# Two-block transformer on one core: products side by side at the stage seams, single modulation tiles through two buffers, layer-norm moments tile by tile

## The chip, the cores and the metric

The kernel runs on one core of a Trainium2 chip. The metric is the device time of one execution in microseconds (us). Engines: PE is TensorE (matmuls), PEld its weight loads, DVE is VectorE, ACT is ScalarE, POOL is GpSimd, SP is SyncE, which here only issues transfers.

## The reference

Two transformer blocks in a row on x of 512 tokens by 1024 features, in float32. The first (two layers) has sparse indexed attention, banded attention, gates and a gated feed-forward; the second has forgetting attention, a multi-scale pool, a state-space mixer, and 16 routed experts. What the change touches:

```python
for l in range(DEPTH):                                   # DEPTH = 2
    mod = c_act @ w_ada[l] + b_ada[l]                    # 6 x 1024 modulation values
    sh_m, sc_m, gt_m, sh_f, sc_f, gt_f = jnp.split(mod, 6, axis=-1)
    h = rms_norm(x, g_mix[l]) * (1.0 + sc_m[:, None]) + sh_m[:, None]
    z = h @ w_in[l] + b_in[l]                            # q, k, v, indices, gates ga, gb
    merged = jax.nn.sigmoid(ga) * y_a + jax.nn.sigmoid(gb) * y_b
    x = x + gt_m[:, None] * (merged @ w_out[l])
    h2 = rms_norm(x, g_ffn[l]) * (1.0 + sc_f[:, None]) + sh_f[:, None]
    gate, up = jnp.split(h2 @ w_gu[l], 2, axis=-1)
    x = x + gt_f[:, None] * ((jax.nn.silu(gate) * up) @ w_down[l])
# second block
h = layer_norm(x) * (1.0 + sc_m) + sh_m
mix = hybrid_mixer(h, ...)                               # attention, pool, ssd, gates, w_out
x = layer_norm(ALPHA * x + g_m * mix, ln_mix_g, ln_mix_b)
h = layer_norm(x) * (1.0 + sc_f) + sh_f
ffn = grouped_moe(h, w_router, ...)
x = layer_norm(ALPHA * x + g_f * ffn, ln_ffn_g, ln_ffn_b)
```

## The kernel before, in words

All activations lie transposed: a tile is 128 features (partitions) by 512 tokens, and x, h and merged have eight tiles each (KC = 8). The program is written out by hand, one instruction stream per engine, with semaphores between them; nothing is scheduled by a planner. The classes `Plan` only number the products, weight units and sums, so that each engine knows what count to wait for.

**Products.** A float32 product is made from three fp32r matmuls per chunk of 128 features: upper weight half by upper h, upper by lower, lower by upper (`passes`, lines 583 to 585). A full product has 8 chunks, 24 matmuls of 128x128 by 512 columns. Products go to two PSUM banks in turn, `lin[p % 2]`; `bank_for(p)` waits until product p-2 was evacuated (`lin_free`). ACT or DVE evacuate.

**Weights.** SP loads one unit of 512 KB (a weight of 1024 by 128) into one of four slots of `ring`; unit n waits until the product that read unit n-4 has ended (line 504). ACT writes the upper half (`upper`, line 1236), POOL the lower half (line 2416), and a product waits for `w_lower`. SP's queue is in order: what waits there holds all behind it.

**Modulation.** `mod` is a vector by matrix product, done on DVE: a tile of 128 by 1024 weights is loaded by SP into `wada` and reduced against `csil` (`modulate`, line 1731). In the gates (8 turns), and in the attention outputs of the second block (8 turns, `attout`), SP loads two tiles at a time, 1 MB (`load_tiles`, line 509), into one buffer, so a load waits until DVE has read the one before. Four tiles belong to a turn. In gate/up one tile belongs to each of the first 16 turns.

**A turn of the gates** has two products of h (gates ga, gb; 24 matmuls each) and two of 12 matmuls (attention outputs). ACT evacuates the first two (line 1309), DVE the third and fourth (lines 2004, 2007), adds them into `merged` (line 2010), then reads the tiles. DVE writes the lower half of merged one turn later (line 1826).

**Seams.** Before mix, gate/up and fd, DVE scales a tile of x, ACT applies gain and shift twice (upper half and whole), and DVE takes the difference (`h_lo`, line 1756); the first product waits for it chunk by chunk. The output products wait in the same way for the last tile of merged.

**Layer norms of the second block** (`layer_norm`): sums of x over the features by eight matmuls with ones (line 623), the mean, centring on DVE, squares of the centred tiles on ACT (line 1472), eight more sums, a root on ACT (line 1248), a reciprocal and scaling on DVE (lines 1761, 1763), an affine step on ACT (line 1264). ln1 stands between the two blocks, ln2 and ln3 between the output products and the router (line 1080, 32 groups of matmuls with h as the stationary operand and 16 columns), ln4 at the end, followed by one store of the output.

Of the kernel before, what the change touches and what calls it, by code (L numbers as in the profile page):

```python
# [9 lines left out]
ACT = mybir.ActivationFunctionType  # L10
# [4 lines left out]
P = 128  # L15
# [76 lines left out]
def att_finished(s):  # L92
# [15 lines left out]
    ("ln1", 1, dict(aux=2)),  # L108
# [7 lines left out]
    ("ln2", 1, dict(aux=2)),  # L116
    ("ln3", 1, dict(aux=2)),
    ("router", 1, dict(aux=5)),
    ("ln4", 1, dict(aux=2)),
# [7 lines left out]
class Stream:  # L127
# [13 lines left out]
    def tiles(self, n):  # L141
        self.ada.append((self.slot(n * D), n))
# [130 lines left out]
def two_blocks(nc, w_all, vec1_all, vec2_all, consts, x_in, pos_in, cond, rel, out):  # L273
    ctx = ExitStack()
    with ctx:
# [206 lines left out]
        def _(sp):  # L482
# [34 lines left out]
            for layer in range(LAYERS):  # L517
                load(LAYER.at("gates", "unit", 0))
                for t in range(8):
                    load(3)  # L520
                    if t == 0:
                        sp.wait_ge(o_free, LAYER.at("mix", "o", 1, layer))
                    load_tiles()
                    load_tiles()
                load(8)
                for t in range(FF_T):
                    load(2)
                    if t < 16:
                        load_tiles()
                load(24)  # L530
            load(25)
            for t in range(8):
                load(2)
                if t == 0:
                    sp.wait_ge(o_free, SECOND.at("att", "o", 8))
                load_tiles()
                load_tiles()
            load(20 + 40 + 16 + 8 - 3)
# [23 lines left out]
        def _(pe):  # L562
# [37 lines left out]

            def half_of_h(p, u, part):
# [15 lines left out]
            def column_sum(a, src, k, ready=None):  # L617
# [6 lines left out]
                if k == KC - 1:  # L624
                    mm.then_inc(aux_full, 1)

# [47 lines left out]
            for layer in range(LAYERS):  # L674
# [60 lines left out]
                make("ka", split)  # L735
                make("ki")
# [124 lines left out]
                for t in range(8):  # L861
                    ready = (lambda k: (sem("m_split"), layer * KC + k + 1)) if t == 0 else None
                    product(at("out", "lin", t), [(at("out", "unit", t), 0, chunks_of(mg_hi, mg_lo, range(KC), ready))])
# [4 lines left out]
                for t in range(FF_T):  # L868
# [1824 lines left out]
```

## Time and profile before

| What | Value |
|---|---|
| Median of three runs | 3703.48 us (3698.95 to 3704.59) |
| Profiled execution, its own time | 3694.89 us |
| Span of its profile | 3693.2 us |
| Mean granted TensorE clock | 0.933 |
| Busy: PE, PEld, DVE, ACT, POOL | 86%, 65%, 41%, 28%, 29% |
| Chain that ended last: PE, DVE, DMA, ACT | 48%, 14%, 5%, 3% |

A row of the timeline gives start, duration, engine, line, operation, output and input; in brackets how long the engine had been idle and who ended that. Clock 1.00 is 2.4 GHz, 0.50 is 1.2 GHz. Matmuls overlap, so their starts (0.227 us apart at full clock) tell more than their durations. The stages of layer 0 lie at 58 to 972 us (gates 372 to 515), of layer 1 at 981 to 1906 (gates 1300 to 1450), the second block from there: attention to 2177, attention outputs to 2285, pool to 2436, ssd to 2788, ssd outputs to 2943, output products to 2987, norms and router to 3063, experts to 3622, combination and last norm to 3693.

### The profile page before, as it was taken

What the parts mean: (1) busy time and instruction counts of PE and PEld (TensorE: products, weight loads), DVE (VectorE), ACT (ScalarE), POOL (GpSimd) and SP (SyncE); (2) the same over time, 40 slices, a digit from 0 to 9 for tenths busy, and PEclk for the clock granted to TensorE, in tenths of its full rate; (3) what the DMA queues carried; (4) which work ended last, traced back from release to release, by engine and by line L of the source; (5) the groups of instructions that cost most, each with busy time, mean ns of one, the idle gap of its engine ahead of it and who ended that gap; (6) DMA issues with size and microseconds to landing.
All of it is one profiled execution on the core that took longest, in us unless ns stands there. A gap on an engine that the chain in (4) does not pass through costs nothing.

```text
span 3693.2 us, 38767 instructions
## 1 busy us (share of the span) xinstructions
PE 3183.1 (86%) x15370; PEld 2406.2 (65%) x15370; DVE 1507.0 (41%) x2585; ACT 1045.4 (28%) x1639; POOL 1059.1 (29%) x523
## 2 busy tenths in 40 slices
PE   4887988999898688899989987788888975999994
PEld 2654766887665466688756766666664545888882
DVE  5776543211267645221124434568782141010003
ACT  3444223223344422322234431233331121000002
POOL 1330333444333033344425523334441111000001
PEclk9997999999999899999999998899999986999997
DMA  5210553433311076243323226233332204989982
GB/s 199 60 41 12 182 184 96 144 113 101 105 57 44 12 280 215 86 145 118 98 81 90 79 94 210 66 103 94 95 97 69 97 17 180 338 329 334 337 329 103
DMA packets 176966, 501.73 MB, mean 136 GB/s; under 512 B 18401, under 2 KB 100449, under 8 KB 159409
## 3 DMA queue, kind: packets, MB, share of 16 engines
q1 hardware_dynamic: 153984, 415.14, 33.5%
q0 software_dynamic: 13344, 49.84, 3.5%
q10 hardware_dynamic: 9488, 34.71, 2.7%
q8 instruction: 99, 1.62, 0.2%
q14 instruction: 51, 0.41, 0.0%
HBM read 464.36 MB, written 35.29 MB: 135 GB/s over the span
## 4 chain that ended last, share of the span: by engine, by line
PE 48%; DVE 14%; DMA 5%; ACT 3%; issue 2%; POOL 0%; DVEq 0%; POOLq 0%; SPq 0%; ACTq 0%
PE banks L1123 9%; PE banks L583 9%; PE banks L585 8%; PE banks L584 8%; PE banks L1145 4%; PE banks L1065 3%; DMA arena<-in_w_all 3%; DVE abuf L2188 2%; PE banks L623 2%; DVE arena L1731 1%; DMA ring<-in_w_all 1%; PE banks L648 1%; PE banks L669 1%; DVE arena L1923 1%; PE banks L658 1%
## 5 line engine op out<-in xcount | busy, mean ns | idle before, releaser
L2416 POOL TENSOR_TENSOR w_lo<-ring,w_hi 128x1024 fp32r<-128x1024 f32 (+2 forms) x363 | 878.8, 2425 | 1609.9 <-ACT w_hi L1236 1609.5
L584 PE MATMUL banks<-h_lo,w_hi 128*128 128x512 f32 x2104 | 838.9, 399 | 0.0
L583 PE MATMUL banks<-hx_hi,w_hi 128*128 128x512 f32 (+1 forms) x1400 | 591.9, 423 | 66.0 <-DVE h_lo L1756 36.9
L585 PE MATMUL banks<-hx_hi,w_lo 128*128 128x512 f32 (+1 forms) x1400 | 558.4, 399 | 0.0
L1236 ACT ACTIVATE w_hi<-ring 128x1024 fp32r<-128x1024 f32 (+2 forms) x363 | 375.9, 1037 | 529.2 <-DMA ring<-in_w_all 507.4
L584 PEld LDWEIGHTS banks<-h_lo,w_hi 128*128 128x128 f32 x2104 | 403.4, 192 | 93.6 <-issue 9.7
L583 PEld LDWEIGHTS banks<-hx_hi,w_hi 128*128 128x128 f32 (+1 forms) x1400 | 270.7, 193 | 176.2 <-issue 79.0
L1123 PE MATMUL banks<-abuf,ring 128*128 128x128 f32 x2944 | 334.7, 276 | 1.4 <-DVE abuf L2366 0.9
L1123 PEld LDWEIGHTS banks<-abuf,ring 128*128 128x128 f32 x2944 | 332.5, 193 | 1.9 <-issue 1.9
L585 PEld LDWEIGHTS banks<-hx_hi,w_lo 128*128 128x128 f32 (+1 forms) x1400 | 269.5, 192 | 61.2 <-issue 0.7
L583 PE MATMUL banks<-hf_hi,w_hi 128*128 128x512 f32 x704 | 279.6, 397 | 24.6 <-DVE h_lo L1756 24.6
L585 PE MATMUL banks<-hf_hi,w_lo 128*128 128x512 f32 x704 | 279.5, 397 | 0.0
L1731 DVE CUSTOM_DVE_ANT_0 arena<-arena 128x1024 f32<-128x1024 f32 x144 | 207.1, 1438 | 161.6 <-DMA arena<-in_w_all 153.2
L1309 ACT ACTIVATE sgs<-banks 128x512 f32<-128x512 f32 x84 | 50.0, 595 | 543.5 <-PE banks L585 496.2
L2033 DVE TENSOR_TENSOR arena<-sgs,banks 128x512 f32<-128x512 f32 x44 | 30.2, 687 | 372.6 <-PE banks L585 372.6
L583 PEld LDWEIGHTS banks<-hf_hi,w_hi 128*128 128x128 f32 x704 | 132.7, 189 | 63.2 <-issue 22.8
L1145 PE MATMUL banks<-arena,abuf 128*128 128x512 f32 x368 | 161.8, 593 | 1.0 <-DMA arena<-in_w_all 1.0
L585 PEld LDWEIGHTS banks<-hf_hi,w_lo 128*128 128x128 f32 x704 | 133.0, 189 | 30.7
L2510 POOL DMA_DIRECT2D made<-abuf x23 | 12.3, 536 | 475.2 <-DVE abuf L2377 475.2
L2020 DVE SCALAR_TENSOR_TENSOR x<-banks,mod,x 128x512 f32<-128x512 f32 x32 | 24.0, 751 | 301.3 <-PE banks L585 301.3
L583 PE MATMUL banks<-hid_hi,w_hi 128*128 128x512 f32 x352 | 143.0, 406 | 3.6 <-DVE hid_lo L2041 3.6
L2377 DVE COPY abuf<-banks 128x512 f32<-128x512 f32 x23 | 15.9, 691 | 301.7 <-PE banks L1145 301.7
(366 smaller groups left out, 4495.9 us busy)
## 6 DMA issues: line engine op xcount, KB each, us to landing
ring<-in_w_all SPq DMA_DIRECT2D x340, 512.0 KB, 3.8
ring<-in_w_all SPq DMA_DIRECT2D x46, 2048.0 KB, 8.1
arena<-in_w_all SPq DMA_DIRECT2D x27, 2048.0 KB, 8.6
arena<-in_w_all SPq DMA_DIRECT2D x48, 1024.0 KB, 4.9
arena<-in_w_all SPq DMA_DIRECT2D x32, 512.0 KB, 4.9
routed<-abuf POOLq DMA_DIRECT2D x1, 12288.0 KB, 47.7
abuf<-routed POOLq DMA_DIRECT2D x24, 512.0 KB, 8.4
made<-abuf POOLq DMA_DIRECT2D x23, 512.0 KB, 7.9
```

The lines of the kernel that those rows point to most:

```text
L583: pe.matmul(bank[0:m, :], upper, hi, start=first, stop=False)
L584: pe.matmul(bank[0:m, :], upper, lo, start=False, stop=False)
L585: return pe.matmul(bank[0:m, :], lower, hi, start=False, stop=last)
L623: mm = pe.matmul(aux, ones, src(k), start=(k == 0), stop=(k == KC - 1))
L1065: mm = pe.matmul(bank, raw_w[(u + 1) % SLOTS][:, k * P:(k + 1) * P], yT[:, k, :], start=(k == 0), stop=(k == 15))
L1123: mm = pe.matmul(bank[:, ct * P:(ct + 1) * P], w[:, k * E_FF + ct * P:k * E_FF + (ct + 1) * P], xT[par][:, k * P:(k + 1) * P], start=(k == ...
L1145: mm = pe.matmul(sc_b[half], hidb[:, k * P:(k + 1) * P], wdown[:, k * D + half * SEQ:k * D + (half + 1) * SEQ], start=(k == 0), stop=(k == 3))
L1236: act.activation(w_hi[s][:, 0:n], raw_w[s][:, 0:n], ACT.Copy).then_inc(w_upper, 1)
L1309: act.activation(sg[n][:, :], lin[p % 2], func, bias=bias).then_inc(lin_free[p % 2], 1)
L1731: mine(dve.tensor_tensor_reduce(w, w, csil, 1.0, 0.0, MUL, ADD, mod_sum[:, n:n + 1]))
L2188: ins = STT(o, c[:, tap:tap + SEQ], gpar(5 * t + tap), o, MUL, ADD)
L2416: pool.tensor_tensor(w_lo[s][:, 0:n], raw_w[s][:, 0:n], w_hi[s][:, 0:n], ALU.subtract)\
```

## The change

- `side_by_side` makes two products chunk by chunk, into both banks, where the first product of a stage waited for its input tiles: mix (ka, ki), output (0, 1), gate/up (0, 1), fd with the first attention product, and the output of the second block. It waits for both banks first.
- `load_tile` loads one modulation tile (512 KB) at a time into one of two halves of `wada`, each with its own semaphore. SP's order changes: in the gates a tile is issued behind each weight load. DVE reads two tiles of a turn ahead of the evacuations of the third and fourth product and two behind; the sum goes straight to `mod`, without the extra addition. The last tile of merged is lowered ahead of the last two reads.
- The layer norms take variance as mean of squares less squared mean; sums of x and of its squares are made tile by tile, as x becomes ready (in ln1 between the down products, in ln2 between the output products, in ln3 as the affine step of ln2 gives tiles), the second sum in the bank `ob`. DVE centres and scales tile by tile.
- The router's logits are made with w_router as the stationary operand, 16 by 512, copied, and turned by four transposes.
- The load of ACT's square-root table, the load and silu of the next c, stand earlier, between output products; the result is stored tile by tile.

```diff
@@ sync
-            def load_tiles():
-                n, ((at, size), tiles) = next(ada)
-                sp.wait_ge(sem("wada_free"), n - 3)
-                sp.dma_start(wada[:, 0:tiles * D], w_all[at:at + size * P].rearrange("(p n) -> p n", p=P))\
-                    .then_inc(sem("wada_in"), 16)
+            def load_tile():
+                n, ((at, size), i) = next(ada)
+                n -= 4
+                if n >= 2:
+                    sp.wait_ge(sem("wada_free"), n - 1)
+                sp.dma_start(wada[:, n % 2 * D:(n % 2 + 1) * D], w_all[at:at + size * P].rearrange("(p n) -> p n", p=P)[:, i * D:(i + 1) * D])\
+                    .then_inc(sem("wada_in%d" % (n % 2)), 16)
@@ gates
+                load(3)
+                sp.wait_ge(o_free, LAYER.at("mix", "o", 1, layer))
+                load_tile()
+                load_tile()
                 for t in range(8):
-                    load(3)
-                    if t == 0:
-                        sp.wait_ge(o_free, LAYER.at("mix", "o", 1, layer))
-                    load_tiles()
-                    load_tiles()
-                load(8)
+                    load()
+                    load_tile()
+                    load()
+                    load_tile()
+                    load()
+                    if t < 7:
+                        load_tile()
+                        load_tile()
+                load(5)
@@ attention outputs
+            load(2)
+            sp.wait_ge(o_free, SECOND.at("att", "o", 8))
+            load_tile()
+            load_tile()
             for t in range(8):
-                load(2)
-                if t == 0:
-                    sp.wait_ge(o_free, SECOND.at("att", "o", 8))
-                load_tiles()
-                load_tiles()
+                load()
+                load_tile()
+                load()
+                load_tile()
+                if t < 7:
+                    load_tile()
+                    load_tile()
@@ tensor
+            def side_by_side(p, u, chunks, widths=(P, P)):
+
+                pe.wait_ge(w_lower, STREAM.units[u + 1][4])
+                pair = [bank_for(p), bank_for(p + 1)]
+                for k, (hi, lo, ready) in enumerate(chunks):
+                    for n, m in enumerate(widths):
+                        mm = passes(pair[n], u + n, k * m, m, (hi, lo, None if n else ready), k == 0, k == KC - 1)
+                        if k == KC - 1:
+                            mm.then_inc(lin_full[(p + n) % 2], 1)
...
-            layer_norm("ln2", 1)
-            layer_norm("ln3", 2)
-            pe.wait_ge(sem("h_ready"), KC)
+                for k in ([t - 1] if t < 7 else [6, 7]):
+                    column_sum(at("ln2", "aux"), lambda k: x[:, k, :], k, lambda k: pe.wait_ge(sem("x_mixed"), k + 1))
+                    square_sum(lambda k: moe[:, k, :], k, lambda k: pe.wait_ge(sem("moments"), k + 1))
+            for k in range(KC):
+                column_sum(at("ln3", "aux"), lambda k: x[:, k, :], k, lambda k: pe.wait_ge(sem("x_affine"), k + 1))
+                square_sum(lambda k: merged2[:, k, :], k, lambda k: pe.wait_ge(sem("moments"), KC + k + 1))
@@ vector, gates
+                    modulate_beside(16 + 4 * t, v1)
+                    modulate_beside(17 + 4 * t, v1)
                     taken(dve, p)
                     produced(dve, p + 2)
                     TT(tmp[:, :], sg[0][:, :], lin[(p + 2) % 2], MUL).then_inc(lin_free[(p + 2) % 2], 1)
...
-                    modulate_beside(16 + 4 * t, 2, v1)
-                    modulate_beside(18 + 4 * t, 2, v1)
-                lower_merged(layer * KC, mg_lo, merged, mg_hi, 7)
+                    if t == 7:
+                        lower_merged(layer * KC, mg_lo, merged, mg_hi, 7)
+                    modulate_beside(18 + 4 * t, v1)
+                    modulate_beside(19 + 4 * t, v1)
```

DVE in a turn of the gates, before (mg_lo is the lower half of merged, the ISA rows with arena are the reads of modulation tiles, tmp and sgs take the third and fourth product):

```order
L1826 TENSOR_TENSOR mg_lo_63<-arena,mg_hi_62 128x512 [waits m_upper,dve_steps]
L2004 TENSOR_TENSOR tmp<-sgs,banks 128x512 [waits lin_full1,lin_free1]
L2007 TENSOR_TENSOR sgs<-sgs,banks 128x512 [waits lin_full0,lin_free0]
L2010 TENSOR_TENSOR arena<-tmp,sgs 128x512 [waits lin_free0,lin_free1]
L1731 ISA arena<-arena 128x1024 [waits wada_in]
L1731 ISA arena 128x1
L1731 ISA arena<-arena 128x1024 [waits dve_steps]
L1731 ISA arena 128x1
L1737 TENSOR_TENSOR mod<-arena,vec 128x2 [waits dve_steps]
```

The same turn in the change:

```order
L1906 TENSOR_TENSOR mg_lo_63<-arena,mg_hi_62 128x512 [waits dve_steps,m_upper]
L1806 ISA arena,mod<-arena,vec 128x1024 [waits wada_in0]
L1806 ISA mod 128x1
L1806 ISA arena,mod<-arena,vec 128x1024 [waits dve_steps,wada_in1]
L1806 ISA mod 128x1
L2086 TENSOR_TENSOR tmp<-sgs,banks 128x512 [waits dve_steps,lin_full1,lin_free1]
L2089 TENSOR_TENSOR sgs<-sgs,banks 128x512 [waits lin_full0,lin_free0]
L2092 TENSOR_TENSOR arena<-tmp,sgs 128x512 [waits lin_free0,lin_free1]
L1806 ISA arena,mod<-arena,vec 128x1024 [waits wada_in0]
L1806 ISA mod 128x1
L1806 ISA arena,mod<-arena,vec 128x1024 [waits dve_steps,wada_in1]
L1806 ISA mod 128x1
```

Two of the four reads, and their waits for the tiles, now stand between mg_lo and the evacuation of the third product (tmp); the additions into mod are gone.

SP around the same turn, before (ring is a weight unit, arena a load of modulation tiles; lin_full is the end of the product that frees the slot):

```order
L504 DMA ring<-in_w_all 128x1024 [waits lin_full0]
L504 DMA ring<-in_w_all 128x1024 [waits lin_full1]
L504 DMA ring<-in_w_all 128x1024 [waits lin_full0]
L509 DMA arena<-in_w_all 128x2048 [waits wada_free] x2
L504 DMA ring<-in_w_all 128x1024 [waits lin_full0]
```

The same place in the change:

```order
L505 DMA ring<-in_w_all 128x1024 [waits lin_full0]
L512 DMA arena<-in_w_all 128x1024 [waits wada_free] x2
L505 DMA ring<-in_w_all 128x1024 [waits lin_full0]
L512 DMA arena<-in_w_all 128x1024 [waits wada_free]
L505 DMA ring<-in_w_all 128x1024 [waits lin_full1]
L512 DMA arena<-in_w_all 128x1024 [waits wada_free]
L505 DMA ring<-in_w_all 128x1024 [waits lin_full0]
```

Single tiles stand behind each weight load, and two behind the third, which waits for the second product of a turn.

SP at the end of the gates in the change (128x8x128 are the units of the output products):

```order
L505 DMA ring<-in_w_all 128x8x128 [waits lin_full0]
L512 DMA arena<-in_w_all 128x1024 [waits wada_free]
L505 DMA ring<-in_w_all 128x8x128 [waits lin_full1]
L512 DMA arena<-in_w_all 128x1024 [waits wada_free]
L505 DMA ring<-in_w_all 128x8x128 [waits lin_full0]
```

The last tile is issued behind the weight that waits for output product 0 (lin_full1).

## Rows read from the trace of the kernel before

**Rows 1.** Waits of PE by releaser: total us, times, longest.

```profile
PE banks L583 <- DVE h_lo L1756: 61.4, 23, 16.3
PE banks L583 <- DVE pooled_lo L2157: 30.5, 4, 13.1
```

**Rows 2.** Windows by stage: length, busy of each engine (instructions), clock, DMA share, GB/s.

```profile
2247.30:2254.92 7.62, 7.62 (x25) 6.10 (x26) 2.62 (x5) 0.00 (x0) 1.52 (x1) 0.72 0.40 153
384.53:510.08 125.55, 117.63 (x506) 95.28 (x505) 81.87 (x95) 32.62 (x40) 49.98 (x20) 0.99 0.57 203
1306.25:1444.50 138.25, 120.74 (x505) 96.72 (x505) 79.16 (x95) 32.62 (x40) 49.65 (x20) 0.95 0.71 266
510.08:539.21 29.13, 18.31 (x73) 14.63 (x73) 10.97 (x20) 6.49 (x8) 10.03 (x4) 0.82 0.67 230
2197.40:2285.56 88.16, 72.53 (x290) 57.93 (x289) 40.98 (x62) 15.73 (x18) 28.29 (x12) 0.90 0.56 201
```

**Rows 3.** Timeline of PE: ends of products in gates and attention outputs, next starts.

```profile
473.24 0.39 PE L584 MATMUL banks<-h_lo,w_hi 128*128 128x512 f32 x1
473.46 0.39 PE L585 MATMUL banks<-hx_hi,w_lo 128*128 128x512 f32 x1
...
480.82 0.50 PE L583 MATMUL banks<-hx_hi,w_hi 128*128 128x512 f32 x1 [1.53 <-DVE tmp L2004]
...
2247.30 0.79 PE L583 MATMUL banks<-att_hi,w_hi 128*128 128x512 f32 x1 [4.51 <-DVE arena L2122]
```

**Rows 4.** Landings: lone weight 473.9; tiles in gate/up; weights 2206.4; 1 MB (page).

```profile
DMA to landing us min/median/max: 3.5/3.5/3.5
...
DMA to landing us min/median/max: 4.2/4.8/5.1
...
DMA to landing us min/median/max: 5.8/6.2/6.6
...
arena<-in_w_all SPq DMA_DIRECT2D x48, 1024.0 KB, 4.9
```

**Rows 5.** Timeline of DVE and POOL: tile reads, evacuation, a lower weight half.

```profile
473.43 1.22 DVE L1731 CUSTOM_DVE_ANT_0 arena<-arena 128x1024 f32<-128x1024 f32 x1
...
480.09 0.67 DVE L2004 TENSOR_TENSOR tmp<-sgs,banks 128x512 f32<-128x512 f32 x1
...
1540.91 2.38 POOL L2416 TENSOR_TENSOR w_lo<-ring,w_hi 128x1024 fp32r<-128x1024 f32 x1 [1.18 <-ACT w_hi L1236]
...
1542.24 2.14 DVE L1731 CUSTOM_DVE_ANT_0 arena<-arena 128x1024 f32<-128x1024 f32 x1 [0.18 <-DVE arena L2033]
```

**Rows 6.** Timeline at the entry to gate/up, layer 1: ACT, then PE.

```profile
1514.14 1.28 ACT L1433 ACT_TABLE_LOAD   x1
1516.51 1.28 ACT L1248 ACT_TABLE_LOAD   x1
...
1524.93 0.77 PE L583 MATMUL banks<-hf_hi,w_hi 128*128 128x512 f32 x1 [10.58 <-DVE h_lo L1756]
...
1540.87 0.39 PE L585 MATMUL banks<-hf_hi,w_lo 128*128 128x512 f32 x1
```

**Rows 7.** Timeline at the entry to mix, layer 1: first product's end, head root.

```profile
991.87 0.40 PE L585 MATMUL banks<-hx_hi,w_lo 128*128 128x512 f32 x1
...
999.29 0.59 ACT L1253 ACTIVATE rstd<-banks 128x512 f32<-128x512 f32 x1
```

**Rows 8.** Chain of waits, in order of time: start, us, what.

```profile
1909.59 8.81 PE banks L623 x16
...
2988.73 7.15 PE banks L623 x16
...
3007.74 3.37 DVE rstd L1761
...
3049.26 13.85 PE banks L1080 x64
...
3657.54 9.01 PE banks L623 x16
```

More of the change, by code:

```diff
@@ L141, in tiles @@
     def tiles(self, n):
-        self.ada.append((self.slot(n * D), n))
+        slot = self.slot(n * D)
+        self.ada += [(slot, n)] if n == 4 else [(slot, i) for i in range(n)]
     def unit(self, last, *copies, raw=False):
@@ L733, in index_scores @@
                         mm.then_inc(sem("ix_full"), 1)
-                make("ka", split)
-                make("ki")
+                side_by_side(lin_of("ka"), at("mix", "unit"), of_h(split))
                 head_norm("ka")
@@ L860, in _ @@
                     product(p + 3, [(u + 2, 4 * P, chunks_of(attb_hi, attb_lo, range(4)))])
-                for t in range(8):
-                    ready = (lambda k: (sem("m_split"), layer * KC + k + 1)) if t == 0 else None
-                    product(at("out", "lin", t), [(at("out", "unit", t), 0, chunks_of(mg_hi, mg_lo, range(KC), ready))])
+                side_by_side(at("out", "lin"), at("out", "unit"),
+                             chunks_of(mg_hi, mg_lo, range(KC), lambda k: (sem("m_split"), layer * KC + k + 1)))
+                for t in range(1, 8):
+                    if t > 1:
+                        product(at("out", "lin", t), [(at("out", "unit", t), 0, chunks_of(mg_hi, mg_lo, range(KC)))])
                     for k in ([t - 1] if t in range(1, 7) else [6, 7] if t == 7 else []):
@@ L1774, in layer_norm, with centre @@
                 read(dve, a)
[L1775 to L1778 removed]
+                mine(TT(rstd[:, :], tmp[:, :], tmp[:, :], MUL))
+                dve.wait_ge(sem("var_full"), n + 1)
+                mine(STT(rstd[:, :], ob, 1.0 / D, rstd[:, :], MUL, SUB))
+                tell(TS(rstd[:, :], rstd[:, :], 0.0, LN_EPS, MAX, ADD), sem("var_done"))
+                def centre(k):
+                    TT(dst[:, k, :], x[:, k, :], tmp[:, :], SUB).then_inc(sem("centred"), 1)
+                centre(0)
+                dve.wait_ge(sem("root_done"), n + 1)
+                mine(dve.reciprocal(rstd[:, :], rstd[:, :]))
+                for k in range(KC):
+                    if k + 1 < KC:
+                        centre(k + 1)
+                    dve.wait_ge(sem("centred"), n * KC + k + 1)
+                    TT(dst[:, k, :], dst[:, k, :], rstd[:, :], MUL).then_inc(sem("scaled"), 1)
+                    if lower is not None and k >= 2:
+                        lower(k - 2)
+                if lower is not None:
+                    lower(KC - 2)
+                    lower(KC - 1)
             def rotate(a, src, dst):
```

189 lines of the change are left out of this document (112 added, 77 removed).

## The prediction

> **What bounds the kernel now.** I read the engine that waits first. The page's waits of TensorE say who ends its idle time: at the seams between stages it stands until the first split tiles of h are written (61.4 us over 23 waits), and in the pooling stage for VectorE (30.5 us) [rows 1]. Then the windows by stage: in the gates of layer 0, turns 1 to 7, TensorE is busy 117.6 of 125.5 us at a clock of 0.99; in those of layer 1 120.7 of 138.3, with one long DMA of zeros beside it; from the last turn's second product to the end of the second output product only 18.3 of 29.1; in the attention outputs 72.5 of 88.2 at 0.90 [rows 2]. So there is something to win at the seams and in the attention outputs, and little in the gates, where almost any new wait is a loss.
>
> **The gates (term 1).** The modulation tiles are read by VectorE. Their transfers stand on SP behind weight loads that wait for a product to end. In the new order, tiles 4t and 4t+1 are issued behind a weight load that waits for the *second* product of turn t (call its end B), and VectorE reads both *before* it evacuates the third product. The first product of the next turn needs that bank. Before, tiles stood on SP at the same place, but VectorE read them after the evacuation.
>
> Before, B ended at 473.46 + 0.39 = 473.85 and the next turn began at 480.82 [rows 3]: 7.0 us, of which 5.4 are the third and fourth product (24 matmuls at 0.227, the step of the same rows) and 1.5 a wait.
> Now, from B = 0:
> - SP issues the weight at 0.0 and, at 0.4 an issue (my estimate), the first tile at 0.4; the second waits on the read of tile 4t-1, at about 0.8. A 512 KB load alone lands in 3.5 us; a tile behind a weight in 4.8; two weights behind a tile of 1 MB land 5.8 and 6.6 after their issue [rows 4]. So: weight 3.5, first tile 5.2, second 6.3.
> - ScalarE writes its upper half in about 1.1 and GpSimd lowers it in 2.38, from 4.8 to 7.2.
> - A tile's read takes 1.22, but 2.14 when it starts at 1542.24 while GpSimd works from 1540.91 to 1543.29: it ends 1.1 after GpSimd does. The evacuation, which takes one operand from PSUM, keeps its 0.67 [rows 5]. So the first read ends at 8.3, the second at 9.6, the evacuation at 10.4; the next turn begins at 10.5. The halves of the last merged tile are made before the first tile lands and hide in this.
> - TensorE stands 10.5 - 5.4 = 5.1 us. After 4.5 us of standing, the product at 2247.30 ran at a clock of 0.72 and took 7.6 instead of 5.5 [rows 2, 3]: 2.1 more.
>
> Per turn 10.5 - 7.0 + 2.1 = +5.6. A turn becomes 23.8 us. Layer 0: 7 x 23.8 = 166.6 against 125.5, **+41**. Layer 1: 166.6 against 138.3 is +28, and the zeros share the DMA engines as before; what they cost before is 138.3 - 125.5 = 12.8, of which I take 8: **+36**. Ends: without a read behind GpSimd the second read ends at 7.6 and the turn begins at 8.4, +1.4 a turn and no clock loss (+10 and +4 with the zeros); or +8 a turn if both reads wait.
>
> The Trainium skill ("SBUF — State Buffer", section "SBUF: two separate sides") says that VectorE with two SBUF inputs and GpSimd take the shared port pair in turn, each for a whole instruction. By that rule the second read may also be shut out, if GpSimd gets in between; the trace shows one such wait per read at most.
>
> **Behind the gates (term 2).** The two output products start when both banks are free, 11.2, run 48 matmuls in 11.2 + 2.1 and end at 24.5; before, the second ended at 29.1 [rows 2]. But the last tile is issued on SP behind the weight of output 4, which waits for output 0. It lands about 4.9 after the pair, its read takes 1.3, and the residual of output 0 is queued behind it on VectorE, then its square on ScalarE, then the column sum. TensorE stands 7.6 and loses 2.1 again. 24.5 + 7.6 + 2.1 + 1 = 35 against 29.4: **+5.8** per layer, +12 in all (from +1, when the pair starts at 9.2, to +12).
>
> **Entry to gate/up (3).** Table loads of 1.28 and the silu of c stand between the last sum and the root; they end 3.65 after they begin; hoisted, the first product starts 3.4 earlier. Tiles of h come every 1.41 us, six matmuls take 1.37, so both products end about 13.2 after the start, against 1541.26 - 1524.93 = 16.3 [rows 6]. **-6.3** per layer, -13 (ends: -8, -14). The Trainium skill ("ScalarE: Activation LUTs", section "What ACT_TABLE_LOAD costs") puts a switch at about 2.66 us with its drain; here the next instruction starts right behind the 1.28, so the trace decides; by the page two hoists would give 2.8 more.
>
> **Entry to mix (4).** The pair saves 2.9 us of TensorE, but the slot of the first product is freed 2 us later (before at 992.3 [rows 7]), its next weight lands 3.5 later, and ScalarE splits that weight before the head root (before at 999.29): it would start at 998.8. The pair's gain waits there: **-1** for both layers (0 to -3).
>
> **Layer norm 1 (5).** Eight square sums (8.81) and the squares leave the chain at 1909.59 [rows 8]; 5.4 come back between the down products. VectorE now centres and scales per tile, 2.0 us a tile instead of 1.41, but fd and the first attention product share that time. The next stage then stands on ScalarE, which empties the bank of that product only behind the fd chain. Estimate **-9** (-4 to -14).
>
> **Layer norms 2, 3, router (6).** From 2988.73 to the end of the logits at 3063.10 it is 74.4 us: four rounds of sums, two reciprocals of 3.37, the logits 13.85 [rows 8]. The first two rounds move between the output products (+12.9 there, of which 1.4 is the pair's wait for a bank and 1 the wait for x). What is left behind the last product: 6.2 to the root, 3.4, eight tiles; third and fourth round together 16 (16 sums at 0.89 to 1.1), behind them 2.7, 3.4, eight tiles at 1.25 with the logits beside them, 2 for copy and transposes: about 47. 76 - 47 - 13 = **-16** (-10 to -20).
>
> **Layer norm 4 (7).** The sums begin with the first x tile, 5 us before 3657.54 [rows 8]; output leaves per tile: 3693 becomes 3688, **-5** (-2 to -8).
>
> **Attention outputs and pooling (8).** Before, one buffer of 1 MB made a turn 14.7 (88.2/6) [rows 2]. Now the second tile of each turn waits on SP for that turn's first product; tracing tile by tile with landings of 3.5 to 5 and one GpSimd wait per turn I get turns of 10.9 and 15.9 in alternation, 13.4: **-8** (-16 to +4). The last read ends 8 us earlier, so of the 13.1 at the first pooling wait [rows 1] **-8** (-4 to -9). The Trainium skill ("DMA: Bandwidth & Descriptors", section "Measured") advises transfers of 1 MiB and more; here a half takes 3.5 against 4.9 for the whole [rows 4], and by that rule alone, four halves one after the other with their reads (4 x 4.8) would make a turn of 19, which only the second buffer avoids.
>
> Sum: 41 + 36 + 12 - 13 - 1 - 9 - 16 - 5 - 8 - 8 = +29. The profiled execution took 3694.9, 8.6 below the median of the runs shown (3703.5). So 3724 by the profile, **3733** by the median.
>
> **The rivals.**
> - *The gates' reads do not meet GpSimd, and the idle stays short of what lowers the clock.* Then terms 1 and 2 are 10 + 4 + 1 = +15, and the sum is -45: 3659. Decisive: whether the second tile's read ends before about 7.7 after B. For it: 1.5 us of standing never lowered the clock in these gates (0.99). Against it: GpSimd's work is released by the weight issued just ahead of the tiles, so the two meet each turn.
> - *The norms do not pay.* VectorE takes 2.0 us per tile where ScalarE set 1.41, and the sums are still read last; terms 5 to 7 halve and the attention outputs stay at 14.7: +29 + 15 + 8 = +52, 3756.
> - *The terms cancel.* If the gates cost half (+40 in all), the sum is about -20 to 0; a little of this lies within 0.2%.
>
> **How the numbers follow.** Forecast (slower by 15 to 45) 0.50; norms do not pay 0.12; reads do not meet, and all between it and the forecast on the fast side, 0.30; within 0.2% (7 us, about what a measurement of this kernel can tell from none) 0.08. So faster 0.30, same 0.08, slower 0.62. The range takes in most of the fast rival and the slow one: 3665 to 3768. The likeliest case alone spans 3718 to 3748.
>
> **What would show it.** In the gates of the changed profile: turns near 23.8 us; TensorE's wait for tmp near 5 us, some fifteen times, with a lower clock; reads of 2 us or more beside GpSimd; a wait of 7 to 8 us after the output pair. At gate/up, a root without a table load ahead of it. From the last output product to the logits near 47 us. I am wrong if the turns stay under 19.5 us: then term 1 falls, and the kernel is faster.

## The result, and the profile after

The changed kernel takes 3764.4 us (median of 4 runs, 3756.4 to 3769.0) against 3701.2 for the kernel before in the same series. The ratio is 1.0172, 95% interval 1.0156 to 1.0187: **slower by 63 us**, where I forecast slower by 30. The sign was right. The time lies inside the stated 3665 to 3768 us, but near its upper end and outside the band of 3718 to 3748 that I called likeliest: about half of the loss was missing from my sum. The profiled execution has a span of 3767.4 us against 3693.2, +74.2.

The waits of TensorE come first, as in [rows 1] (columns: total us, times, longest). I call one such wait a stand.

```profile
PE banks L599 <- DVE tmp L2086: 84.4, 14, 10.8
PE banks L599 <- DVE h_lo L1819: 48.9, 5, 15.4
...
PE banks L599 <- DVE sgs L2089: 24.5, 2, 12.6
PE banks L599 <- DVE pooled_lo L2242: 22.7, 4, 7.0
...
PE banks L649 <- ACT h L1463: 19.1, 4, 9.1
PE banks L599 <- POOL w_lo L2504: 18.6, 2, 12.3
...
PE banks L599 <- DVE arena L2205: 16.3, 4, 4.2
```

The seams shrank (61.4 to 48.9) and so did pooling (30.5 to 22.7). The wait for tmp, the evacuation of the third product of a gates turn, is 84.4 us in 14 waits. Three waits are new and large: 24.5 us ahead of the two output pairs (L2089), 8.8 and 9.1 of the 19.1 us behind them (L1463), and 12.3 of the 18.6 us for a lower weight half (L2504). The first of these stands in place of one that the kernel before had, 10.8 and 10.1 us of output product 0 for the last tile of merged:

```profile
PE banks L583 <- DVE mg_lo L1826: 20.9, 2, 10.8
```

The windows by stage (length, busy time by engine, clock, DMA share, GB/s): gates of layer 0 and of layer 1 from the end of turn 0 to the end of turn 7, then a stretch of the attention outputs with the first products of pooling.

```profile
391.74:560.82 169.08, 132.37 (x504) 105.82 (x504) 76.61 (x84) 32.93 (x41) 49.30 (x21) 0.86 0.47 154
1364.56:1543.95 179.39, 131.65 (x504) 105.25 (x504) 74.62 (x84) 34.08 (x42) 49.89 (x21) 0.84 0.57 206
...
2292.00:2395.00 103.00, 86.51 (x355) 69.43 (x354) 61.63 (x64) 19.79 (x23) 38.94 (x15) 0.94 0.66 227
```

The same seven turns took 125.5 us at 0.99 and 138.2 at 0.95 before [rows 2]. TensorE now runs the same products in 132 us instead of 118, at a granted clock of 0.86, and stands for the rest.

Where the 74 us arise, by the time at which the same product starts or ends in both traces (forecast: what my terms put there):

| from ... to | before ends at | after ends at | change | forecast |
|---|---|---|---|---|
| start to end of gates turn 0, layer 0 | 389.97 | 391.74 | +1.8 | -0.5 |
| gates turns 1 to 7 | 515.50 | 560.82 | **+43.5** | +41 |
| to the first gate/up product | 590.50 | 646.09 | **+10.3** | +2.4 |
| to mix of layer 1 | 981.49 | 1033.66 | -3.4 | -2.9 |
| to end of gates turn 0, layer 1 | 1311.69 | 1364.56 | +0.7 | -0.5 |
| gates turns 1 to 7 | 1449.90 | 1543.95 | **+41.2** | +36 |
| to the first gate/up product | 1524.93 | 1629.19 | **+10.2** | +2.4 |
| to the fourth attention product's end | 1971.76 | 2074.31 | -1.7 | -11.9 |
| to the first attention output product | 2179.18 | 2282.95 | +1.2 | 0 |
| to the last attention output product's end | 2285.56 | 2384.74 | -4.6 | -8 |
| to the first pooled product | 2316.72 | 2413.31 | -2.6 | -8 |
| to the end of the logits | 3063.10 | 3142.57 | -17.1 | -16 |
| to the end | 3693.2 | 3767.4 | -5.3 | -5 |

The gates, router and norm 4 came as forecast within a few us. Four places did not: twice between gates and gate/up, once at the forget seam (fd), once between the attention outputs and pooling.

A turn of the gates, in the chain of waits (start us, us, what):

```profile
483.99 5.43 DMA arena<-in_w_all
...
489.44 2.28 DVE arena L1806
...
491.91 1.28 DVE arena L1806
...
493.42 0.70 DVE tmp L2086
```

Tile, long first read, short second read, evacuation, next turn: the row that the forecast drew. The next turn starts 10.6 us after the second product's end (483.61 to 494.17), forecast 10.5.

The last turn is different. The chain from its second product to the first column sum:

```profile
556.00 10.86 DMA arena<-in_w_all
566.88 3.27 DVE arena L1806
...
570.34 1.28 DVE arena L1806
...
572.46 0.69 DVE sgs L2089
...
586.32 5.40 DMA arena<-in_w_all
591.74 1.28 DVE arena L1806
...
593.58 0.76 DVE x L2103
594.37 0.64 ACT h L1463
```

The tile takes 10.86 us, twice that of other turns. ScalarE's queue shows what shares the DMA engines with it (timeline of ACT, same turn):

```profile
555.55 0.35 ACTq L1456 DMA_DIRECT2D x<-in_x_in  x1
```

That is the 2 MB load of x back from HBM, issued half a microsecond before the tile. It stood at the same place in the program before, but no evacuation waited for the tile then. My working never looked at ScalarE's queue.

The forget seam (timeline of ACT, POOL and PE):

```profile
2009.59 1.06 ACT L1269 ACTIVATE w_hi<-ring 128x1024 fp32r<-128x1024 f32 x1 [3.23 <-DMA ring<-in_w_all]
...
2043.52 0.56 POOL L2540 DMA_DIRECT2D f_rows<-arena  x1 [35.21 <-DVE arena L2146]
2045.68 1.12 POOL L2545 DMA_DIRECT2D arena<-f_rows  x2 [1.60 <-DMA f_rows<-arena]
2046.81 2.35 POOL L2504 TENSOR_TENSOR w_lo<-ring,w_hi 128x1024 fp32r<-128x1024 f32 x1
...
2049.31 0.77 PE L599 MATMUL banks<-hx_hi,w_hi 128*128 128x512 f32 x1 [12.29 <-POOL w_lo L2504]
```

The upper half of the weight of attention product 1 is ready at 2010.7. GpSimd could lower it then, but first in its queue stands a wait for the fd rows, 35 us long. Product 0 was moved ahead of that chain by the pair; product 1 stands behind it, and the first four products end no earlier.

### The profile page after: what moved, and what is told of

The parts are those of the page before. It is cut to its first block, busy times and chain, and to the rows that moved or that the text cites. A ratio compares the mean times of both kernels' runs of the same rounds, so it can differ in the third digit from the quotient of the medians.

```text
span 3767.4 us, 38674 instructions
## 1 busy us (share of the span) xinstructions
PE 3207.1 (85%) x15326; PEld 2422.0 (64%) x15326; DVE 1510.8 (40%) x2518; ACT 1045.5 (28%) x1639; POOL 1056.2 (28%) x523
## 4 chain that ended last, share of the span: by engine, by line
PE 67%; DVE 19%; DMA 6%; ACT 4%; issue 3%; POOL 1%; SPq 0%; DVEq 0%; ACTq 0%; POOLq 0%
PE banks L599 15%; PE banks L601 14%; PE banks L600 14%; PE banks L1154 8%; DMA arena<-in_w_all 5%; PE banks L1176 4%; PE banks L1087 3%; DVE arena L1806 2%; DVE abuf L2273 2%; PE banks L649 1%; DVE arena L2003 1%; PE banks L681 1%; PE banks L702 1%; DVE arena L2002 1%; PE banks L662 1%
## 5 line engine op out<-in xcount | busy, mean ns | idle before, releaser
L2504 POOL TENSOR_TENSOR w_lo<-ring,w_hi 128x1024 fp32r<-128x1024 f32 (+2 forms) x363 | 876.7, 2417 | 1723.9 <-ACT w_hi L1269 1723.4
L600 PE MATMUL banks<-h_lo,w_hi 128*128 128x512 f32 x2104 | 850.7, 404 | 0.0
L599 PE MATMUL banks<-hx_hi,w_hi 128*128 128x512 f32 (+2 forms) x1400 | 607.4, 434 | 148.5 <-DVE tmp L2086 84.4
L601 PE MATMUL banks<-hx_hi,w_lo 128*128 128x512 f32 (+2 forms) x1400 | 570.3, 407 | 0.0
L600 PEld LDWEIGHTS banks<-h_lo,w_hi 128*128 128x128 f32 x2104 | 412.9, 196 | 99.4 <-issue 10.5
L599 PEld LDWEIGHTS banks<-hx_hi,w_hi 128*128 128x128 f32 (+2 forms) x1400 | 280.4, 200 | 255.6 <-issue 93.5
L601 PEld LDWEIGHTS banks<-hx_hi,w_lo 128*128 128x128 f32 (+2 forms) x1400 | 277.1, 198 | 64.5 <-issue 0.3
L1806 DVE CUSTOM_DVE_ANT_0 arena<-arena,vec 128x1024 f32<-128x1024 f32 x96 | 166.5, 1734 | 285.1 <-DMA arena<-in_w_all 280.4
L2598 POOL DMA_DIRECT2D made<-abuf x23 | 12.3, 536 | 474.9 <-DVE abuf L2466 474.9
L2103 DVE SCALAR_TENSOR_TENSOR x<-banks,mod,x 128x512 f32<-128x512 f32 x32 | 23.8, 750 | 299.4 <-PE banks L601 299.0
L601 PE MATMUL banks<-hid_hi,w_lo 128*128 128x512 f32 x352 | 138.3, 393 | 0.0
```

Source lines behind the costliest of these rows:

```text
L599: pe.matmul(bank[0:m, :], upper, hi, start=first, stop=False)
L600: pe.matmul(bank[0:m, :], upper, lo, start=False, stop=False)
L601: return pe.matmul(bank[0:m, :], lower, hi, start=False, stop=last)
L1806: mine(dve.tensor_tensor_reduce(w, w, csil, 1.0, start, MUL, ADD, dst))
L2504: pool.tensor_tensor(w_lo[s][:, 0:n], raw_w[s][:, 0:n], w_hi[s][:, 0:n], ALU.subtract)\
```

## The experiments

Each kernel was timed against the kernel before on the same chip (3699.1, 3702.6, 3698.9 and 3697.2 us in the four series). Profiles of code that is identical up to there reach the end of the first gates up to 7 us apart, so effects of less than 10 us are read from the stage that the edit touches, and the medians stand beside. For these small effects the stage is the better evidence.

**e1, reads behind the evacuations.**

```diff
                         lower_merged(layer * KC, mg_lo, merged, mg_hi, t - 1)
-                    modulate_beside(16 + 4 * t, v1)
-                    modulate_beside(17 + 4 * t, v1)
                     taken(dve, p)
...
                         lower_merged(layer * KC, mg_lo, merged, mg_hi, 7)
+                    modulate_beside(16 + 4 * t, v1)
+                    modulate_beside(17 + 4 * t, v1)
                     modulate_beside(18 + 4 * t, v1)
```

> The changed kernel, with the reads of tiles 4t and 4t+1 in the gates moved back behind the two evacuations on VectorE; the two buffers and the order of the loads stay. Theory (the evacuation of the third product stands behind the reads): the wait for tmp falls from 5.2 to under 2 us, a turn from 23.9 to 16.5 to 18.5 us and runs at the full clock, so the gates of both layers take 75 to 95 us less; the output pair starts within 2 us of the last product instead of 12.6, but stands for its last chunk or for the last read later. In all 3764 becomes about 3660 (3645 to 3690). Rival (it is the two half transfers and their order on SP that are late): the turns stay above 21 us, and the kernel above 3730.

Measured: **3640.3 us** (3629.5 to 3642.2), 0.9834 of before (0.9817 to 0.9852). That is 124 us less than the changed kernel by moving two lines, and below the 3645 to 3690 that I expected: the gates of both layers give about 103 us (expected 75 to 95), the earlier start of the two output pairs 22. The window over the gates of layer 0, from the third product of turn 0 to the end of turn 7:

```profile
379.60:507.57 127.97, 127.97 (x568) 103.83 (x566) 77.20 (x85) 37.70 (x47) 61.01 (x23) 1.00 0.67 216
```

TensorE does not stand at all, at full clock. The window holds 0.9 us of attention, the last 48 matmuls of turn 0 (11.2 us, as in the changed kernel) and seven turns: 16.6 us a turn, where before it was 17.9. In layer 1, beside the zeros, two stands of 6.8 and 2.0 us are left. The output pair starts 1.6 us behind the last product, not 12.6. So the order on VectorE was the loss, and the two buffers with single tiles, read behind the evacuations, also remove the wait of 1.5 us a turn that the kernel before had.

**e2, x loaded later.**

```diff
-                    if t == 7:
-                        act.dma_start(x[:, :, :], x_kept if layer else x_in).then_inc(sem("x_back"), 16)
                     upper_to(u + 5)
                 upper_merged(layer * KC, mg_hi, merged, 7)
+                act.dma_start(x[:, :, :], x_kept if layer else x_in).then_inc(sem("x_back"), 16)
```

> The changed kernel, with the 2 MB load of x back from HBM issued behind the upper half of the last merged tile, some 18 us later, instead of in the middle of the last gates turn. Theory (this load shares the DMA engines with the tiles of the last turn, whose reads stand ahead of the evacuation): the tile that landed 10.9 us after its wait began lands 4 to 6 us earlier, the output pair starts 6 us earlier in each layer, and the kernel takes 9 to 14 us less: 3752. Rival (the two tiles are late by the queue of SP alone): within 3 us of the changed kernel.

Measured: 3755.3 us (3751.2 to 3756.9), 9 less than the changed kernel, at the low end of the 9 to 14 expected. In its chain of waits the tile's transfer falls from 10.86 to 5.60, behind it the first read is unchanged:

```profile
551.90 5.60 DMA arena<-in_w_all
...
557.53 3.29 DVE arena L1805
```

The pair waits 7.35 and 7.02 us instead of 12.58 and 11.95. The load of x was the missing 5 us a layer ahead of the pair.

**e3, the last tile ahead of the weight.**

```diff
                     load()
                     load_tile()
+                    if t == 7:
+                        load_tile()
                     load()
-                    load_tile()
+                    if t < 7:
+                        load_tile()
```

> The changed kernel, with the last modulation tile (31) issued on SP right behind tile 30, ahead of the weight load that waits for output 0. Theory (the residual of output 0 is queued on VectorE behind the read of that tile): TensorE's stand of 8.8 us behind the output pair falls to under 2.5, the next product runs at the full clock (6.1 instead of 8.4 us), and each layer gains 8 to 11 us: 3745. Rival (the tile lands late through contention, or the square on ScalarE is what is late): a gain under 6 us in all.

Measured: 3739.4 us (3739.2 to 3740.3), 25 less than the changed kernel. From the start of the output pair to the first gate/up product it is 62.0 and 62.3 us instead of 72.7 and 73.3. The chain behind the pair is now residual, square, sum, with no tile in it:

```profile
580.03 0.76 DVE x L2106
...
580.82 0.64 ACT h L1466
...
581.60 1.10 PE banks L652 x2
```

This stand I had in the forecast (7.6 us and 2.1 of clock); it costs 10.7 and 11.0.

**e4, one more unit lowered ahead of the forget chain.**

```diff
-            lower_to(u)
+            lower_to(u + 1)
             pool.wait_ge(sem("f_done"), 1)
```

> The changed kernel, with one more weight unit lowered by GpSimd ahead of the wait for the forget chain (fd), the one of attention product 1. Theory (the pair of fd and attention product 0 gained nothing since product 1 waits for its lower half, queued on GpSimd behind the DMA of the fd rows): the wait of 12.3 us behind the pair falls to under 1, product 2 becomes what waits, and the last of the first four products ends 8 to 12 us earlier: 3754. Rival (the attention's start hangs on the fd rows and the causal segments instead): the products move, but the first attention step moves by under 3 us, and so does the kernel.

Measured: 3753.7 us (3750.6 to 3758.1), 11 less. Of its waits of TensorE at the seam, in place of the one of 12.3 us:

```profile
PE banks L599 <- POOL w_lo L2504: 5.0, 2, 2.7
PE banks L671 <- DVE arena L2150: 2.9, 1, 2.9
```

From fd to the first attention step it is 44.3 us instead of 50.6. In the later kernels with this edit it is 43.4 to 44.5, in those without it and with the pair 50.3 to 51.9. So the edit gives 6 to 7 us, and the rest of the 11 lies ahead of the seam, in stages that the edit does not touch. The expected 8 to 12 was too much: half of it turned into later waits, 2.9 us for the acs rows and 2.3 and 2.7 for the lower halves of products 2 and 3.

**e5, the same reordering in the attention outputs.**

```diff
-                for k in range(16 + 4 * t, 18 + 4 * t):
-                    modulate_beside(k, v2)
                 gated("attout", t, False)
-                for k in range(18 + 4 * t, 20 + 4 * t):
+                for k in range(16 + 4 * t, 20 + 4 * t):
                     modulate_beside(k, v2)
```

> The changed kernel, with the reads of tiles 4t and 4t+1 in the attention outputs moved behind the evacuation of the turn's second product on VectorE. Theory (as in the gates: the evacuation stands behind the reads): the wait of 4.0 us at every second turn goes, a turn falls from 13.9 to 11 to 12 us, 12 to 22 us over the stage, of which the first pooling wait takes 3 to 8 back since the last read now ends later: 3764 becomes 3752 (3744 to 3760). Rival (the transfers, 3 MB a turn, set the 13.9): the waits move from one product to another and the kernel stays within 4 us.

Measured: 3758.4 us (3754.9 to 3762.6), 6 less. The time is in the expected range, the mechanism half missed: the waits spread and hardly shrink (16.3 us in 4 became 14.7 in 6), although the products behind them run faster. From the first output product to the first pooled one it is 125.4 instead of 130.4. Waits of TensorE over that stage:

```profile
PE banks L599 <- DVE arena L2205: 14.7, 6, 3.3
PE banks L599 <- DVE pooled_lo L2240: 7.4, 1, 7.4
```

Here VectorE itself is the limit in part: two reads in a row run beside GpSimd. In the changed kernel (timelines of DVE and POOL):

```profile
2338.64 3.32 DVE L1806 CUSTOM_DVE_ANT_0 arena<-arena,vec 128x1024 f32<-128x1024 f32 x1 [0.31 <-DMA arena<-in_w_all]
...
2342.16 3.15 DVE L1806 CUSTOM_DVE_ANT_0 arena<-arena,vec 128x1024 f32<-128x1024 f32 x1 [0.19 <-DVE mod L1806]
...
2338.50 2.37 POOL L2504 TENSOR_TENSOR w_lo<-ring,w_hi 128x1024 fp32r<-128x1024 f32 x1 [7.90 <-ACT w_hi L1269]
2341.05 3.17 POOL L2504 TENSOR_TENSOR w_lo<-ring,w_hi 128x1024 fp32r<-128x1024 f32 x1 [0.18 <-ACT w_hi L1269]
```

In e5 two such reads still stand ahead of the evacuation, since the turn's last tiles land that late: they take 3.10 and 3.12 us from 2335.96, 3.24 and 3.34 from 2348.99.

**e6, the five edits together.** (Diff: the five above.)

> The changed kernel with all five edits: reads behind the evacuations in the gates and in the attention outputs, the load of x late, the last tile ahead of the weight, one more lowering ahead of the forget chain. With the first edit alone it took 3640. From there the last tile takes away the 9.0 and 8.5 us stands behind the output pair (16 to 18), the lowering 10, the attention outputs 12; the late load of x gives nothing more, since no evacuation stands behind the reads of the last turn now: 3600 (3588 to 3612). If the gains overlap (the same stand counted twice, or the tiles become late elsewhere), it stays above 3615.

Measured: **3622.1 us** (3620.3 to 3626.6), 0.9785 of before (0.9765 to 0.9805). That is 18 under e1, not 40, and the expectation of 3588 to 3612 fell. The parts, against e1: from the output pair to gate/up 3.0 and 3.2 us, at the forget seam 6.7, in the attention outputs 2.8, together 15.7. The last tile gives less here, since in e1's order tiles 30 and 31 are issued after the last product anyway, and now meet the late load of x (chain of waits, behind the pair):

```profile
508.34 7.81 DMA arena<-in_w_all
```

**e7, tiles as before.** (The changed kernel with the loading, the order and the reads of the modulation tiles taken from the kernel before.)

> The changed kernel with the modulation tiles as before (one buffer, pairs of tiles, reads behind the evacuations), the side-by-side products, norms and router as changed. Theory (all of the loss comes from the tiles' part, and the rest pays by what the traces show): against before the output pairs give 13, the gate/up seams 12 to 13, norms 2, 3 and router 16, norm 4 7, the entry to mix and the forget seam 0 to +3: about 3653 (3643 to 3668). If it is above the 3640 that the changed kernel takes with its reads behind the evacuations, two buffers are worth the difference. Rival (the pairs or norms lose too): over 3680.

Measured: 3653.4 us (3651.9 to 3655.1), 0.9866 of before (0.9846 to 0.9886), as expected. So the tiles' part costs 111 us net, and all the rest of the change gains 49. Against e1 the two buffers with single tiles, read behind the evacuations, are worth 13.

**e8, norms, router and table loads alone.** (e7 with each pair made as two products again.)

> The kernel before with only the norms' and router's part and the hoisted table loads (no pairs, tiles as before). Theory: the hoisted loads give 3.4 in each layer, norms 2, 3 and the router 16, norm 4 7, norm 1 about nothing (it gives 7.5 at the seam and takes 4.5 between the down products; then GpSimd's queue decides): 3699 becomes 3670 (3662 to 3678). Rival (the norms do not pay): 3690 or more.

Measured: 3664.3 us (3660.9 to 3669.8), 0.9892 of before (0.9871 to 0.9912). From the first output product of the second block to the start of the logits it is 90.4 us, where it was 106.4; from there to the end 12 less, 5 of it in the logits themselves (8.6 us for 13.8). From the last layer's down stage to fd 147.6 against 148.5: norm 1 gives nothing net. The pairs are the 11 us between e8 and e7.

**e10, e6 with the load of x at its old place.** (The edit of e2 taken out.)

> The version with all five edits, less one: the load of x is issued at its old place, in the middle of the last gates turn. Theory (with the reads behind the evacuations the two last tiles are issued only when that turn is over, so the late load of x now shares the DMA engines with them: a tile took 7.8 us there): the stand of 6.1 us behind the output pair falls to 1 to 3 in each layer, 3622 becomes 3614 (3610 to 3619). Rival (the stand has another cause): within 3 us of 3622.

Measured: 3629.1 us (3626.0 to 3635.1), not under e6 but 7 above. The expectation fell. TensorE stands 8.4 and 7.9 us behind the pairs, against 6.1 and 5.4 in e6. The timeline of ACT shows why:

```profile
502.01 0.34 ACTq L1459 DMA_DIRECT2D x<-in_x_in  x1
...
511.85 1.06 ACT L1272 ACTIVATE w_hi<-ring 128x1024 fp32r<-128x1024 f32 x1 [8.08 <-DMA ring<-in_w_all]
512.82 0.62 ACT L1353 ACTIVATE mg_hi<-arena 128x512 fp32r<-128x512 f32 x1
```

The early load holds up a weight unit, and ScalarE waits for that unit (8.08 us) ahead of the upper half of the last merged tile. VectorE's lowering of it, the four reads and the last tiles' issues follow. The 2 MB meet something wherever they stand.

**e11, VectorE as changed, SP turned.**

```diff
                     load()
                     load_tile()
-                    load()
                     if t < 7:
                         load_tile()
                         load_tile()
+                    load()
```

> The changed kernel with VectorE's order as changed, and only the queue of SP turned: in the gates tiles 4t and 4t+1 are issued ahead of the weight load that waits for the second product of turn t, not behind it. Theory (the stand needs both: the tiles land late, and the evacuation stands behind their reads): the tiles land before that product ends, the turns fall from 23.9 to 16.6 to 19 us without an edit on VectorE, and the kernel takes 3640 to 3680. Rival (the order on VectorE alone decides, through GpSimd's lowering or the wait for the read before): the turns stay above 21 us.

Measured: 3728.7 us (3723.1 to 3732.7), 36 under the changed kernel. The theory's 3640 to 3680 fell, and the rival's sign came: from turn 2 on the turns of layer 0 take 21.2 to 22.5 us, each with the same stand of 2.96. VectorE from the second product's end (at 426.6) to the evacuation, and GpSimd beside it:

```profile
428.83 2.47 DVE L1906 TENSOR_TENSOR mg_lo<-arena,mg_hi 128x512 fp32r<-128x512 f32 x1 [0.83 <-ACT mg_hi L1350]
431.22 1.27 DVE L1806 CUSTOM_DVE_ANT_0 arena<-arena,vec 128x1024 f32<-128x1024 f32 x1
...
432.69 1.28 DVE L1806 CUSTOM_DVE_ANT_0 arena<-arena,vec 128x1024 f32<-128x1024 f32 x1 [0.19 <-DVE mod L1806]
...
434.20 0.69 DVE L2086 TENSOR_TENSOR tmp<-sgs,banks 128x512 f32<-128x512 f32 x1 [0.22 <-DVE mod L1806]
...
428.35 2.39 POOL L2504 TENSOR_TENSOR w_lo<-ring,w_hi 128x1024 fp32r<-128x1024 f32 x1 [3.11 <-ACT w_hi L1269]
```

The tiles are there; the reads are at their short 1.28. But the lowering of the last merged tile, 0.69 us alone, meets GpSimd and ends at 431.3, and 2.7 us of reads follow. So the late landing was about 2.3 of the 5.2 us and the reads' place on VectorE, with GpSimd beside it, the rest. The place brings a stand by itself. The late landing does not: e1 has the changed kernel's order on SP, and TensorE does not stand in layer 0.

**e12, e10 with tile 4t+3 of the attention outputs ahead of the weight.**

```diff
                 load()
                 load_tile()
-                load()
                 load_tile()
+                load()
```

> The version before this call's first (all edits, load of x early), with tile 4t+3 of the attention outputs issued ahead of the weight load that waits for the next turn's first product. Theory (that tile lands last and its read holds back the evacuation, 1.1 to 2.4 us a turn in six turns): the waits go, the stage takes 6 to 10 us less, and the first pooling wait of 9.1 us shrinks or stays: about 8 us under the first kernel of this call. Rival (GpSimd's lowering beside the reads sets the turn, 3.2 us for a read instead of 1.28): less than 3 us.

Measured: 3620.3 us (3616.2 to 3621.3), 9 under e10. From the first attention output to the first pooled product it is 120.9 us instead of 125.5, under the 6 to 10 expected; three waits of 1.1 to 2.2 are left, and the first pooling wait is 10.8 us for 10.0. The rest of the 9 is not in this stage.

**e13, all edits.** (e12 with the edit of e2.)

> The last kernel (all edits, tile 4t+3 of the attention outputs ahead of the weight) with the load of x late again. With the load early it took 3620; the traces of the two versions that differ in it alone show 8.3 and 6.5 us of stand around the output pairs with the load early against 7.2 and 6.5 late in sum of what is ahead and behind, and a product that starts the slower the longer the stand; by the medians the late load is worth 7: 3613 (3608 to 3620). If it is above 3620, the 7 us between the two versions were noise.

Measured: **3617.0 us** (3610.1 to 3621.5), 0.9779 of before (0.9764 to 0.9795). It beats both kernels, by 80 and 147 us, but is not told apart from e12 (0.9783, 0.9767 to 0.9800). The sums of stands in that expectation were taken wrongly for the early load: ahead of and behind the pairs they are 10.2 and 8.9 early (e10) against 7.2 and 6.5 late (e6). The medians put the place of the x load at 3 us here and at 7 between e10 and e6. The stage itself agrees better: from the last gates product to the first gate/up product, both layers together, the late load is 5.9 us shorter in e6 than in e10 and 5.6 shorter in e13 than in e12.

## Why the direction came true, and where the size failed

The gates decided the sign, and their mechanism was right. Of the 45 us by which the profiles differ from my sum, 16 lie behind the gates, 11 in and ahead of them, 10 at norm 1 and fd, and 9 between the attention outputs and pooling.

**Term 1, the gates: right.** Forecast 23.8 us a turn and a stand of 5.1, measured 24.2 (169.08/7) and 5.1 to 5.4; +43.5 where I said +41. (The +5.6 a turn of the working gives 23.5 on the 17.9 before, not 23.8; the sum used the larger figure.) One more detail than I had: the lowering of merged also waits for GpSimd (2.47 us for 0.69), and hides. In layer 1 it is +41.2 for +36: the first two turns stand 10.8 and 10.0 us, while the DMA engines move 403 GB/s there, zeros for the most part, and an evacuation now waits for the tiles (median landing 7.3 us in these turns for 4.9). I had put 8 us on the zeros; with 179.4 against 169.1 in layer 0 it is 10.3. e1 removes the waits, but for 8.8 us in layer 1.

**Term 2, behind the gates: the step that failed most.** I wrote that "the two output products start when both banks are free, 11.2" after B, which is the row of an ordinary turn. The last turn carries the 2 MB load of x besides, and its tile lands in 10.86 instead of 5.43. The pair starts 18.0 us after B (555.41 to 573.40), not 11.2, which is 6.8 of the miss. The stand for tile 31 was right in kind and larger in size (8.8 and 2.3 for 7.6 and 2.1). Together +13.7 a layer (10.3 and the 3.4 that the hoisted loads give back) where I had +5.8: 16 us of the 45 that my sum lacked. e2 and e3 show both parts.

**Term 3, gate/up: right.** The hoist gives 3.4 (the wait falls from 10.57 to 7.17), the pair 3.4, in layer 0.

**Term 4, entry to mix: nearly.** Forecast -1 for both, measured +1.8 and +0.7, within what identical code varies there.

**Term 5, norm 1 and fd: wrong, by 10 us.** I counted 9 us from a chain that starts earlier. It does: from the last down product to fd 13.9 us instead of 21.4. But the sums between the down products take 5 us of it back, the forget chain starts only when the pair ends (12.96 us, where fd alone took 10.7), and I wrote that "fd and the first attention product share that time" without asking what product 1 waits for. It waits for GpSimd, whose queue stands at the fd rows. e4 shows it: with that wait gone the seam is 6.4 us shorter.

**Term 8, attention outputs and pooling: one gain counted twice.** I took 8 us for shorter turns and 8 more from the first pooling wait. Before, the first pooled product hung on a chain from the last tiles through VectorE, which no product entered in its last 30 us (chain of waits, before):

```profile
2298.14 4.93 DMA arena<-in_w_all
...
2304.48 1.24 DVE arena L1731 x2
...
2315.37 1.31 DVE pooled_lo L2157 x2
...
2316.72 0.80 PE banks L583
```

A last read 8 us earlier brings that product forward by 8 in all; shorter turns alone only lengthen the wait in front of it. From the first attention output product to the first pooled one it was 137.5 us and is 130.4: -7.2, where the two entries made -16. The turns themselves were nearly right: stands of 4.0 to 4.2 at every second turn as drawn, 13.9 us a turn for 13.4 forecast and 14.7 before, -4.6 over the six turns for -8. The same stand then falls once more in pooling (4.05 us ahead of 2394.23, and a slow product behind it), where I had none. The wait for pooled_lo did fall from 13.1 to 5.2, in part only because the products ahead of it end later.

**Terms 6 and 7: right.** From the last output product's end to the end of the logits 45.2 us for "about 47"; -17.1 for -16 and -5.3 for -5. e8 shows gains of that size without the pairs and the tiles.

**The rivals.** The fast one (reads do not meet GpSimd) is out: the first read of a turn is 2.3 to 3.3 us. "The norms do not pay" gave a time near the measured one (3756), for the wrong reason: e8 shows that with the table loads they pay 38 us (33 to 48) by themselves.

## What to carry to other kernels

An engine that reads late data must not stand, in program order, between a full bank and its evacuation: two lines moved on VectorE made 124 us. When a read is made to gate a product, look at every queue for what shares its transfer in each turn, the last above all, since a load that was hidden before is in the chain now. When a product is moved ahead of a chain, ask what the next product waits for on each engine's queue; and where two terms end at the same wait, follow its chain and count the gain once.

## What the runs showed of the hardware

- A VectorE read with two SBUF operands takes 1.28 us alone and 3.3 when GpSimd's subtraction started 0.15 us ahead of it; a 128x512 subtraction of VectorE becomes 2.47 instead of 0.69. GpSimd's own instruction grew from 2.37 to 3.17 when it started while such a read ran. The evacuations with a PSUM operand kept 0.69. The Trainium skill ("SBUF — State Buffer", section "SBUF: two separate sides") calls this an exclusive lock held for a whole instruction; the two reads in a row of 3.32 and 3.15 agree, where I had allowed for one such wait per turn.
- Stands of 2.96 us in every turn (e11) leave a granted clock of 0.89 over the gates of layer 0, stands of 5.2 us (the changed kernel) 0.86, no stand (e1) 1.00. Behind a stand of 2.96 us a turn's 72 matmuls take 18.2 us in most turns and up to 19.5, though one turn of layer 1 took 16.6; behind 5.2 us they take 18.6 to 19.5, without a stand 16.6. The forecast had only rows at 1.5 us, which cost nothing, and at 4.5 us [rows 2, 3].
